# Half-width stationaries and a reordered attention in a four-layer transformer kernel

## The reference

```
s = einsum('btghd,bngd->bghtn', q, k) * scale ; p = softmax(where(mask, s, NEG))
o = einsum('bghtn,bngd->btghd', p, v)                     # values
S = exp(b_last) * S + einsum('bhsd,bhsv->bhdv', k * exp(b_last - b), v)   # HGRN2 state
```

## Time and profile before

| what | us |
|---|---|
| median of 3 runs | 1297.23 (1297.09 to 1297.38) |
| the profiled execution | 1299.27 |
| its span, first to last instruction | 1297.5 |
| TensorE busy (matmul) | 1274.1, 98% of the span |
| VectorE busy | 854.9, 66% |
| ScalarE busy | 688.8, 53% |

### The profile page before, as it was taken

The page is one execution under the profiler, slowest core; times in us unless marked ns, Lnnn a source line. Parts: engine busy times, 40 slices in busy tenths (PEclk is TensorE's granted clock), DMA queues, the critical chain, the costliest instruction groups (busy, mean ns, idle before and its releaser), DMA issues.

```text
span 1297.5 us, 18881 instructions
## 1 busy us (share of the span) xinstructions
PE 1274.1 (98%) x7413; PEld 1089.5 (84%) x7413; DVE 854.9 (66%) x1171; ACT 688.8 (53%) x1168; POOL 107.6 (8%) x112
## 2 busy tenths in 40 slices
PE   6999999999999999999999999999999999999998
PEld 5978888887888888888888888888888788888887
DVE  5876665657645766666767766666666866766664
ACT  6775454446665544445554555555454554555552
POOL 1102000003200400001011030000021010100000
PEclk9999999999999999999999999999999999999999
DMA  9535656556522565654652155565555423555550
GB/s 361 195 125 194 212 171 208 170 188 207 167 97 98 195 210 179 198 192 141 251 196 66 67 178 184 190 194 194 173 193 206 163 68 101 190 187 190 192 193 35
DMA packets 62328, 224.45 MB, mean 173 GB/s; under 512 B 7192, under 2 KB 7328, under 8 KB 62240
## 3 DMA queue, kind: packets, MB, share of 16 engines
q1 hardware_dynamic: 59616, 214.23, 49.1%
q0 software_dynamic: 1904, 6.82, 1.6%
q10 hardware_dynamic: 720, 2.19, 0.5%
HBM read 222.16 MB, written 1.05 MB: 172 GB/s over the span
## 4 chain that ended last, share of the span: by engine, by line
PE 90%; DVE 4%; ACT 3%; issue 1%; DMA 1%; POOL 0%; ACTq 0%; DVEq 0%; POOLq 0%
PE ps L364 18%; PE ps L311 17%; PE ps L316 17%; PE ps L315 17%; PE ps L372 8%; PE ps L476 4%; PE ps L511 2%; PE ps L534 2%; PE ps L362 1%; PE ps L439 1%; PE ps L852 1%; ACT whi L1039 1%; DVE wlo L1623 1%; DVE small L1708 1%; ACT scr L1094 1%
## 5 line engine op out<-in xcount | busy, mean ns | idle before, releaser
L1623 DVE TENSOR_TENSOR wlo<-raw,whi 128x1024 fp32r<-128x1024 f32 (+1 forms) x386 | 459.9, 1213 | 238.7 <-ACT whi L1039 237.3
L1039 ACT ACTIVATE whi<-raw 128x1024 fp32r<-128x1024 f32 (+1 forms) x393 | 404.2, 1047 | 281.3 <-PE ps L364 173.1
L364 PE MATMUL ps<-XT,whi 128*128 128x512 f32 x1024 | 279.4, 394 | 0.0
L364 PEld LDWEIGHTS ps<-XT,whi 128*128 128x128 f32 x1024 | 177.2, 189 | 25.4
L311 PE MATMUL ps<-whi,HT_hi 128*128 128x512 f32 x448 | 175.4, 392 | 0.5 <-DVE HT_lo L1812 0.5
L316 PE MATMUL ps<-whi,HT_lo 128*128 128x512 f32 x448 | 174.4, 389 | 0.0
L315 PE MATMUL ps<-wlo,HT_hi 128*128 128x512 f32 x448 | 174.3, 389 | 0.0
L372 PEld LDWEIGHTS ps<-XT,wlo 128*128 128x128 f32 x896 | 137.4, 189 | 18.9
L372 PE MATMUL ps<-XT,wlo 128*128 128x256 f32 x896 | 142.5, 281 | 0.0
L311 PE MATMUL ps<-whi,XT 128*128 128x512 f32 (+1 forms) x304 | 121.0, 398 | 5.4 <-DVE wlo L1623 3.0
L316 PE MATMUL ps<-whi,XT 128*128 128x512 f32 (+1 forms) x304 | 116.8, 384 | 0.0
(11 more groups left out here) (261 smaller groups left out, 1688.9 us busy)
## 6 DMA issues: line engine op xcount, KB each, us to landing
raw<-in_w_m SPq DMA_DIRECT2D x152, 512.0 KB, 4.2
raw<-in_w_n SPq DMA_DIRECT2D x108, 512.0 KB, 4.3
raw<-in_w_c SPq DMA_DIRECT2D x48, 512.0 KB, 4.5
raw<-in_w_o SPq DMA_DIRECT2D x32, 512.0 KB, 3.7
raw<-in_w_kv SPq DMA_DIRECT2D x16, 512.0 KB, 4.6
raw<-in_w_b SPq DMA_DIRECT2D x16, 512.0 KB, 4.3
raw<-in_w_w SPq DMA_DIRECT2D x16, 512.0 KB, 4.8
raw<-in_w_a SPq DMA_DIRECT2D x12, 512.0 KB, 7.7
```

The lines of the kernel that those rows point to most:

```text
L364: m = pe.matmul(outs[f][:, :], hi[:, j, at(f)], both, start=(k == 0), stop=(k == KT - 1))
L1039: act.activation(whi[:, g % NSPLIT, 0:w], raw[:, g % NRAW, 0:w], ACT.Copy).then_inc(split_hi, 1)
L1623: dve.tensor_tensor(wlo[:, g % NSPLIT, 0:w], raw[:, g % NRAW, 0:w], whi[:, g % NSPLIT, 0:w].bitcast(F32), ALU.subtract).then_inc(split_lo, 1)
```

## The change

Five edits.

1. `values`: where a head has 64 features (`fa`, `sl`, `sw`), the 128-column stationary of a value product is cut into two of 64 columns, which write PSUM partitions 0 to 63 and 64 to 127 in turn. A step has 8 matmuls instead of 4.
2. `cmp_scores`: the same cut, and both token tiles are now issued at (7, 1), where tile 1 was at (7, 2).
3. In steps 2 to 5 of layers 2 and 3 (`near`), `values(n-1)` stands ahead of `between[(n, 1)]`, that is right before level 2, 4, 5 and 7, where it was last in its iteration. Three half units move from (2, 1), (4, 1), (5, 1) to (2, 0), (4, 0), (5, 0).
4. Both halves of level 0 move from (0, 1) and (0, 2) to behind the second `windows_by_unit`, ahead of `scores(1)`.
5. At the start VectorE clears a 128x128 tile and TensorE multiplies it with itself into bank 4, with nobody reading it: 12 products before the wait for the identity, 2 after the gain transposes, 6 after the first transposes of the tokens, 7 between the first and the second unit of `xq0`.

```diff
@@ attend(..., near=())
+                    rows = min(hd, P)
                     for j in range(nh):
                         h = h0 + j
                         for t in range(kt):
-                            m = pe.matmul(out[:, h * hd:(h + 1) * hd],
-                                          turned(tag, n)[:, (j * kt + t) * P:(j * kt + t + 1) * P],
-                                          V(h, t), start=(t == 0), stop=(t == kt - 1))
+                            for u in range(0, P, rows):
+                                at = (j * kt + t) * P + u
+                                m = pe.matmul(out[u:u + rows, h * hd:(h + 1) * hd], turned(tag, n)[:, at:at + rows],
+                                              V(h, t), start=(t == 0), stop=(t == kt - 1))
...
+                    if n in near:
+                        values(n - 1)
                     if (n, 1) in between:
                         between[(n, 1)]()
...
-                    if n > 0:
+                    if n > 0 and n not in near:
                         values(n - 1)
...
+            pe.wait_ge(ev("blank"), 1)
+            def keep_on(times):
+                for _ in range(times):
+                    pe.matmul(PS[4][:, 0:P], slot(11, P), slot(11, P), start=True, stop=True)
+            keep_on(12)
             pe.wait_ge(ev("ident"), 16)
...
             turn("gcol", 5, [sm("grow", P)[0:KT, :]])
+            keep_on(2)
             turn_norm(0, 0)
-            block_by_token("xq0", "w_a", 1, tok(XT), [0, 1], after_norm(0))
+            keep_on(6)
+            block_by_token("xq0", "w_a", 1, tok(XT), [0, 1], {(0, 1): lambda: keep_on(7), **after_norm(0)})
...
@@ cmp_scores
-                        m = pe.matmul(PS[3][:, at:at + 2 * NCMP], q_pair(h)[:, tt * P:(tt + 1) * P], sm("kcT", 2 * NCMP),
-                                      start=True, stop=True)
+                        for u in range(0, P, HALF):
+                            m = pe.matmul(PS[3][u:u + HALF, at:at + 2 * NCMP],
+                                          q_pair(h)[:, tt * P + u:tt * P + u + HALF], sm("kcT", 2 * NCMP),
+                                          start=True, stop=True)
...
@@ weave
-                    if (n, s) in ((0, 1), (1, 0), (1, 1), (2, 1), (3, 0), (3, 1), (4, 1), (5, 1)) or 6 <= n < 10 and s < 2:
+                    if (n, s) in ((0, 1), (1, 0), (1, 1), (2, 0), (3, 0), (3, 1), (4, 0), (5, 0)) or 6 <= n < 10 and s < 2:
...
@@ other_heads
                     for _ in windows_by_unit(1):
                         pass
+                    for half in range(2):
+                        level(0, half)
                     read_out(f"zT{L}.q1")
...
-                    {(0, 1): lambda: level(0, 0), (0, 2): lambda: level(0, 1),
-                     (1, 1): lambda: level(1), (2, 1): lambda: level(2),
+                    {(1, 1): lambda: level(1), (2, 1): lambda: level(2),
...
-                     (7, 1): lambda: cmp_scores(0), (7, 2): lambda: cmp_scores(1), (8, 1): lambda: hgrn_out(1),
+                     (7, 1): lambda: (cmp_scores(0), cmp_scores(1)), (8, 1): lambda: hgrn_out(1),
...
-                     12: lambda: hgrn_rows(1)}, (6, 6), weave, other_heads)
+                     12: lambda: hgrn_rows(1)}, (6, 6), weave, other_heads, (2, 3, 4, 5))
...
@@ vector
+            dve.memset(slot(11, P), 0.0).then_inc(ev("blank"), 1)
             for tt in range(TT):
                 norm_rows(0, tt, x[:, tt, :])
```

More of the change, by code:

```diff
@@ L498, in out_rows, with attend @@
                 turn(f"{tag}.{tt}", bank + tt, [xn[:, tt, lo + j * P:lo + (j + 1) * P] for j in range(4)])
-            def attend(tags, specs, between, turn_banks=(6, 7), weave=None, first=None):
+            def attend(tags, specs, between, turn_banks=(6, 7), weave=None, first=None, near=()):
                 steps = steps_of(tags)
```

## The result

The changed kernel takes 1302.51 us as the median of 6 runs (1301.72 to 1303.75), against 1298.06 (1297.09 to 1300.41) of the kernel before beside it: ratio 1.0028, 95% interval 1.0018 to 1.0038. It is slower by 0.28%, and the time lies above the stated range of 1292.5 to 1299.5. The profiled execution has a span of 1300.4 us against 1297.5, so the 2.9 us between the two traces are the thing to explain. The forecast between them was -0.9.

A forecast was written before the change was run, and what follows sets the result against it. The prediction took TensorE, busy for 98% of the span, as the bound. Start -2.0, layer 1 -0.7 and reordering +1.8 made -0.9 us, from 1297.2 to 1296.3 us; range of 8 in 10, 1292.5 to 1299.5.

The forecast's parts named there:

- the reordering: Layers 2 and 3: new order with later savings counted in, +0.9 us per layer, +1.8 us for both.
- the new waits: Layers 2 and 3: TensorE waits longer before levels 3 and 6 and for the value bank, 3.75 us per layer.
- the savings behind `scores(7)`: Layers 2 and 3: `cmp_scores` saves 0.47 us and values 5, 6, 7, 10 and 11 save 0.70 per layer.
- the clock is not gained: Rival, at the start: the higher clock is not there, the 2.0 us are lost, 1298.3 us; chance 0.12.
- Start, -2.0: Start: idle products bring the higher clock early, units 1 and 2 take 1.4 us instead of 2.6; -2.0 us.
- Layer 1, -0.7: Layer 1: five isolated value steps with half stationaries gain 0.14 us each, -0.7 us.
- `scores(7)`, +2.1 per layer: Layers 2 and 3, up to `scores(7)`: 0.3 - 0.14 - 1.8 + 1.5 + 0.85 + 1.4 = +2.1 us per layer.
- hand-over arithmetic: Layers 2 and 3: distances from level 2 to 3 and 5 to 6 stay 3.8 and 3.3 us, so waits grow.
- value bank wait: Layers 2 and 3: value step 2 waits until bank 2 is emptied for tile 1, +0.85 us per layer.
- the halves do not overlap: Rival, value steps and `cmp_scores`: 0.060 us per record, 0.96 per value step, 1309 us; chance 0.10, partial overlap included.
- The savings count in full: Rival, layers 2 and 3: the three new waits are absent, 1288.8 us; chance 0.17, half savings included.

The follow-up runs named there:

- e9: The kernel before with only the first twelve idle products and the memset they read, the 2, 6 and 7 others left out: 1299.03 us, ratio 0.9998.
- e5: The changed kernel with value products at full width again, its order, idle products and halves of `cmp_scores` kept: 1307.85 us, ratio 1.0068 to the kernel before.
- e1: The changed kernel with seven idle products in each of the waits before levels 3 and 6: 1300.29 us, ratio 1.0005 to the kernel before.
- e2: The changed kernel with value steps, half units and level 0 back in the old order; halves and idle products stay: 1294.48 us, ratio 0.9961 to before.
- e4: The changed kernel with the three half units back at (2, 1), (4, 1), (5, 1): 1296.92 us, ratio 0.9979 to the kernel before.
- e7: e2 with value step 4 issued right before level 7 and no half unit moved: 1294.78 us, ratio 0.9964 to the kernel before.
- e10: e7 with level 8 issued ahead of the half unit at (6, 0) instead of behind it: 1292.77 us, ratio 0.9953 to the kernel before.
- e11: e4 with level 8 issued ahead of the half unit at (6, 0): 1294.83 us, ratio 0.9970 to the kernel before.
- e8: e2 with only the three half units moved, to (2, 0), (4, 0), (5, 0): 1301.30 us, ratio 1.0016 to the kernel before.
- e3: The kernel before with all the idle products at the start and nothing else: 1297.25 us, ratio 0.9983.
- e12: e2 with only one half unit moved, from (2, 1) to (2, 0): 1298.17 us, ratio 0.9994 to the kernel before.

## Why the prediction was wrong

The step that failed is the reordering, +1.8 us for both layers in the sum, where the traces have +5.3 up to `scores(10)` (2.29 and 2.98). Two things were missing in it. It priced the new waits as waits and put what TensorE's clock does behind them at nothing: the clock fell behind one of them in each layer, 2.3 us. And it took the savings behind `scores(7)`, -1.17 per layer, as savings of the whole, without asking what the first half unit of `hg` waits for: ScalarE's copies took 1.5 us of them. The one pause that the prediction had cited as evidence that the clock holds, 1.01 us at 669.62, is shorter than the new ones and stands at another place; that row does not speak for them. The rival "the clock is not gained" looked only at the start. Point by point, with the forecast first:

- Start, -2.0: -1.76. Tile 1 forecast near 20.2, measured 20.44. Right in mechanism, but lucky in one point. The prediction had the first twelve products raise the clock by 7.21 and gave the others no gain. In e9, with the twelve alone, the transposes at 7.20 run at the full rate and the clock falls in the pause of 2.11 us behind them, so the products in the pauses are needed.
- Layer 1, -0.7: -0.22. An isolated value step from 16 records costs what was forecast (0.61 and about 0.09 going in, 0.70), but TensorE meets ScalarE's copies earlier. The same view as the earlier trace rows of the changed kernel has one wait more: those for copies are 0.16 and 0.24 us, where the kernel before has a single one of 0.16, and the last, for exponentials, is 0.55 against 0.54:

```profile
372.52 1.06 PE L476 MATMUL ps<-const,scr 128*128 128x128 f32 x8 [0.16 <-ACT scr L1071]
...
377.83 0.66 PE L476 MATMUL ps<-const,scr 128*128 128x128 f32 x4 [0.24 <-ACT scr L1071]
...
395.40 0.66 PE L476 MATMUL ps<-const,scr 128*128 128x128 f32 x4 [0.55 <-ACT scr L1111]
```

From one `scores` to the next the gain is 0.07 to 0.15 us in four of the six steps with narrow values, nothing in one and -0.07 in one, the two with the waits of 372.52 and 377.83; a step behind them is 0.13 longer. With full width and the rest unchanged layer 1 takes 32.19 us (e5), so the -0.22 is what the halves bring there. Why the steps with waits gain nothing was not taken apart further and stays open.
- `scores(7)`, +2.1 per layer: +1.86 and +1.88 with the clock held (e1), +2.69 and +3.37 with its fall. The hand-over arithmetic was right: level 2 to 3 measured 3.77 us (forecast 3.8), level 5 to 6 3.23 (3.3), waits of 1.75 and 1.57, a value bank wait of 0.67 (0.85; the rows that it was worked out from give 4.30 - 3.57 = 0.73). The missing term, the clock, is +0.83 and +1.49.
- Behind `scores(7)`, -1.17 per layer to the end, of which -0.89 (`cmp_scores` and three value steps) lies ahead of `scores(10)`: -0.40 up to there in both layers. `cmp_scores` did shrink to one stretch of 1.12 us; the rest went into the wait for the `hi` banks. Their chain begins at level 6: two multiplications and a copy on VectorE, a `wlo`, the maxima of `scores(6)`, then ScalarE's exponentials and three copies. From level 6's start to the end of the copies it takes 8.5 us in the kernel before, in e2, e4 and e7, whatever TensorE saves in between (7.56 in the changed kernel, where the `wlo` comes ahead of the multiplications). e10 and e11 show what the wait costs: taken away, it is worth 1.4 and 1.2 us (0.0011 and 0.0009 of the time). In the trace of before the half unit begins at 705.40 without a wait, but only 0.12 us behind the end of the copies, where the gap is 0.10 or 0.11 in the traces in which it waits (e4, e7, the changed kernel). So it had nothing to spare, and a row that the prediction did not use shows it (timeline of ScalarE, before; 703.71 + 1.57 = 705.28):

```profile
703.71 1.57 ACT L1054 ACTIVATE scr<-ps 128x512 f32<-128x512 f32 x3
```

- The rivals: "the halves do not overlap" is wrong (0.03 us per record, as level 0). "The savings count in full" is wrong for this order: all three waits are there. Another order, e10, is 6.8 us faster than the kernel before.

The sum of what was missed, in us: 0.24 at the start, 0.48 in layer 1, 2.3 for the clock, 1.5 behind `scores(7)`, and 0.5 less than forecast in the hand-overs, 4.1 (0.24 + 0.48 + 2.32 + 1.54 - 0.46). With the -0.4 that lies between the stretches of the table these are the 3.8 us between -0.9 and +2.9.

## What to carry to other kernels

When an edit lengthens a wait of TensorE, price the wait and then what follows it: whether the clock is still at its upper level behind it, which one undisturbed profile does not settle. A mean clock of 0.997 where every execution of before has 0.999 or 1.000 is the first line to read, and the granted clock by stretch the second, since the mean can mislead (e9, below). Work that can fill a chain between two engines (here a half unit between a level and the copy of it) belongs inside the chain; moving the half units ahead of it, to gain on a change of shape, lost 6.8 us (e8 against e2). And before counting a saving, look one step further for the transfer or copy that was just in time, by the gap between its end and the start of what needs it: in e10 swapping two pieces gave back 1.4 us that other edits had already earned.

## What the runs showed of the hardware

- TensorE's clock fell from 2.4 to 1.2 GHz behind waits of 1.56 to 1.75 us for a level's copy, but not behind every one: of the 14 such waits in four traces, 8 were followed by a fall (2 of 4 in the changed kernel, 4 of 4 in e5, 2 of 4 in e8, none of 2 in e12). The full rate was back some 3 to 6 us after the wait's end. In the kernel before, with at most 1.01 us of wait, the same stretch stayed at 1.00. Idle products in the waits held the clock (e1), as they did at the start (e3 against e9).
- The length of a wait alone does not decide it. None of the ten waits of 1.77 us for `wlo` at the first half unit (changed kernel, e1, e4, e5 and e11, both layers; 668.28 above) is followed by a fall, and neither is a wait of 1.69 to 1.74 us in layer 0, which every trace has. Below it is in the kernel before, where the granted clock stays at 1.00 behind it. What makes the difference was not separated.

```profile
80.29 1.10 PE L511 MATMUL ps<-scr 128*128 128x256 f32 x4 [1.71 <-ACT scr L1256]
```

- The granted clock of a stretch is not always the rate at which products run: before its first rise the kernel before has 0.43 us per 512 columns under a clock written as 1.00, while in e9, at the same spot and the same 0.43 us, but after an earlier rise (the transposes at 7.20 take 1.09 us instead of 1.97), it is written as 0.50.
- So the column shows e9 at half clock for 10 us, where it shows none of it for the kernel before, and both take the same time (0.9998; mean clock 0.995 to 0.997 against 0.999 to 1.000). The mean clock of a whole execution compares kernels only where their starts agree.
- Half-width products on alternating column halves: 0.03 us from record to record, and about 0.1 us at the change of shape in each direction, in values, levels and `cmp_scores` alike (in layer 1 of the changed kernel 0.09 us going into a value step and 0.61 from its start to that of the next `scores`; the earlier trace rows has 0.060 from record to record where all lie on one half).
